# One planned order for four engines, or an order for each: dilated attention and the branch products of a two-layer block

## The chip, the cores and the metric

One core of one Trainium2 chip. The metric is the device time of one execution in microseconds (us). Before the change it is 3101.1 us, the median of three runs from 3099.65 to 3101.7.

## The reference, cut to what matters

The program is one layer of a mixing block and then one layer of a second block, on 1024 rows of 1024 columns in float32. The change touches a part of the first layer:

```python
qb, kb, vb = ...                        # columns of h @ w_in: 12 heads of 128, in 3 groups of 4
for gi, (window, dil) in enumerate(((128, 1), (512, 4), (2048, 16))):
    o_g, lse_g = _dilated_group(qb[hs], kb[hs], vb[hs], bias[gi], dil, window // (2 * dil))
wgt = softmax(stack(lses), axis=0)      # over the 3 groups
o_b = sum(wgt[..., None] * stack(outs)) # the shares of the groups
merged = gate_a * (o_a @ w_branch_a) + gate_b * (o_b @ w_branch_b)
```

A dilated group is attention in a band: a tile of 128 queries sees up to 256 keys at its dilation, with a bias, a maximum, an exponential and a product with the values.

## The kernel before, in words

Every engine runs a program of its own, and semaphores tie them. Each large matmul is split in three: a float32 operand is cut into a rounded high part and a rest, and `mm3` (L2499 to L2502) issues high*high, high*low and low*high.

**The work of the stage.** It is written as threads, Python generators, each with a version for TensorE, ScalarE, VectorE and SP (the queue that issues the DMAs). `("v", g)` are the columns of the values of group g: `pe_cols` (L1633) makes 8 keys (four column tiles ct by two halves hf), a key being 24 matmuls of 512 columns in two steps of 12, written here as V3.1a and V3.1b for ct 3, hf 1. The two PSUM banks of these keys alternate, so a key waits until the key two before it has been taken out. ScalarE takes out half 0 (L1777), VectorE half 1 (L1919). Then TensorE turns the tile in two or three pieces into bank 7 (`turn`, L1667; R3.0 is piece 0 of ct 3), and VectorE copies each piece out (L1929) before the next may be turned: one bank holds them. `("qk", g)` are 16 keys of queries and keys, taken out by ScalarE (L1760). `("gb", 3)` are 8 keys of a gate (taken out at L1844).

`("att", g)` is the attention of the 8 tiles of a group. For tile i TensorE does the scores S (L1694), VectorE adds the bias, takes the maximum and negates it (L1871, L1875, L1877), ScalarE does four exponentials (L1798), TensorE turns the result T (L1717), ScalarE copies half of it (L1812 or L1817) and VectorE the other half (L1893 or L1899), TensorE multiplies with the values U (L1729), ScalarE copies the output (L1825) and SP stores it. The scores of tile i+1 are issued before T of tile i.

The weights of the column threads come through two slots: SP loads tile n+2 when the last key of tile n is done, ScalarE cuts out the high part (`act_w_split`, L1618), VectorE the low part (`dve_w_split`, L1623), in their places in the threads.

**The order.** `merged` (L76) lays the steps of several threads into one list: step j of n of a thread with the bounds a and b is due at a + (b-a)(j+1)/n, and the earliest due is next. `walk` (L89) goes through such a list and lets each named thread make one step. Four engines walk the same list, each with its own version of the threads:

```python
plan_dil = [merged((("v", 0), 20, 0.0, 44.0), (("att", 0), 34, 36.0, 148.0), ...)]   # L1580
def pe_dilated(t):
    for order in plan_dil:
        walk(order, lambda key: {...}[key[0]](t, key[1]))                             # L1739
```

**The stage behind it.** `plan_br` (L2052) does the same with two threads on TensorE, ScalarE and VectorE. `("br", 0)` is the first branch product: 16 keys of 24 matmuls, of which the first four run together over all of k, fed by the loaded `oT` as ScalarE (L1831) and VectorE (L1835) cut it. VectorE multiplies each with its gate (L2225), for which the load of `mT` must have landed, and splits the next weights (L1623). `("cb",)` weighs the three groups: VectorE's shares (L2175 to L2192) and sums (L2205, L2208, L2211) with GpSimd's help, then eight turns on TensorE (L2104, K0 to K7), whose results ScalarE (L2127) and VectorE (L2169) split. The second branch product waits for the last of them. SP loads in the order of its program: `oT` 0 to 5 (at L2008, the first step of `("gb", 3)`), `oT` 6 and 7 (L2023), `mT` (L2027), the three groups' outputs (L2279), gates and weights.

Of the kernel before, what the change touches and what calls it, by code (L numbers as in the profile page):

```python
# [120 lines left out]
def program(nc, x, wst, wab, cwt, vecs, gate, relb, meta, lam, lruw, cst, onehot, rope, msk, out):  # L121
    with ExitStack() as ctx:
# [388 lines left out]
        for s in range(16):  # L511
            h, part = divmod(s, 2)
            threads = [(("inv", h, part), NINV, 0.0, 1.0)]
# [1043 lines left out]
        def tile_order(first, rest):  # L1557
            res = []
            for g in range(3):
                n = len(tiles(g))  # L1560
                res += [(g, 0, x_) for x_ in first]
                for i in range(n):
                    if i + 1 < n:
# [13 lines left out]
        TN = {k: n for n, k in enumerate(tile_list)}  # L1577

        steps_att = lambda g: 4 * len(tiles(g)) + 2
        plan_dil = [merged((("v", 0), 20, 0.0, 44.0), (("att", 0), 34, 36.0, 148.0), (("v", 1), 20, 44.0, 136.0),  # L1580
                           (("qk", 1), 33, 134.0, 228.0), (("att", 1), 34, 227.0, 348.0), (("v", 2), 20, 228.0, 335.0),
                           (("qk", 2), 33, 333.0, 425.0), (("att", 2), 34, 424.0, 492.0), (("gb", 3), 18, 424.0, 489.0))]


        gbst = [A(BIAS1 + 512 * i, 512) for i in range(4)]
# [149 lines left out]
                yield from pe_cols(t, key, GB0 + key[1], key[2], key[3])  # L1735

        def pe_dilated(t):
            for order in plan_dil:
                walk(order, lambda key: {"qk": pe_qk, "v": pe_v, "att": pe_att, "gb": pe_gb}[key[0]](t, key[1]))  # L1739

        def act_qk(a, g):
            dil = DIL[g]
# [108 lines left out]
            act_o_high(a, 1)  # L1851

        def act_dilated(a):
            for order in plan_dil:
                walk(order, lambda key: {"qk": act_qk, "v": act_v, "att": act_att, "gb": act_gb}[key[0]](a, key[1]))

        def dve_att(v, g):
            todo = tiles(g)
# [94 lines left out]
            dve_o_low(v, 1)  # L1953

        def dve_dilated(v):
            for order in plan_dil:
                walk(order, lambda key: {"qk": dve_qk, "v": dve_v, "att": dve_att, "gb": dve_gb}[key[0]](v, key[1]))

        def sp_qk(sp, g):
            if g == 1:  # L1960
# [54 lines left out]
                    w_load(sp, GB0 + 2 + c)  # L2015

        def sp_dilated(sp):
            for order in plan_dil:
                walk(order, lambda key: {"qk": sp_qk, "v": sp_v, "att": sp_att, "gb": sp_gb}[key[0]](sp, key[1]))
            for kt in (6, 7):  # L2020
                sp.wait_ge(att_mm, (2, kt, "t"))
                sp.wait_ge(oa_in, kt - 6)
                sp.do.dma_start(oT[:, kt, :], sc_o[kt]).then_inc(*oa_in.tick(kt - 5))  # L2023

            sp.wait_ge(att_mm, (2, 7, "s"))
            for cb in range(4):
                sp.do.dma_start(mT[:, 2 * cb:2 * cb + 2, :], sc_h[2 * cb:2 * cb + 2].rearrange("a p n -> p a n")).then_inc(*ga_in.tick(cb))  # L2027
# [21 lines left out]
        br_mm = flow("br_mm", br_keys)  # L2049
        br_done = flow("br_done", br_keys)  # L2050
        br_prod = flow("br_prod", [k for k in br_keys if k[0]])
        plan_br = merged((("br", 0), 17, 0.0, 1.0), (("cb",), 18, 0.28, 1.0))  # L2052
        BA0, BB0 = 42, 46

        def br_bank(k):
# [50 lines left out]
                yield  # L2106

        def pe_branches(t):
            walk(plan_br, lambda key: pe_cb(t) if key[0] == "cb" else pe_br(t, 0))
            for _ in pe_br(t, 1):  # L2110
                pass

# [36 lines left out]
        def act_branches(a):  # L2149
            for kt in range(2, 8):  # L2150
                act_o_high(a, kt)
            walk(plan_br, lambda key: act_cb(a) if key[0] == "cb" else act_br0(a))
            for k in br_keys[16:]:
                _, cb, ct, hf = k
                hs = slice(512 * hf, 512 * hf + 512)
                a.wait_ge(br_done, k)
                a.do.activation(m_hi[2 * cb + ct][:, hs], mT[:, 2 * cb + ct, hs], ACT.Copy).then_inc(*turned_hi.tick(("m", *k[1:])))
                if BN[k] in (17, 20):
                    act_w_split(a, 48 if BN[k] == 17 else 49)
                if BN[k] in (23, 25, 27, 30):  # L2160
                    act_wo_high(a, {23: 50, 25: 53, 27: 51, 30: 52}[BN[k]])
# [66 lines left out]
        def dve_branches(v):  # L2228
            for kt in range(2, 8):
                dve_o_low(v, kt)  # L2230
            walk(plan_br, lambda key: dve_cb(v) if key[0] == "cb" else dve_br0(v))
            def low(k):
                _, cb, ct, hf = k
                hs = slice(512 * hf, 512 * hf + 512)
# [1719 lines left out]
```

## Time and profile before

| | us |
|---|---|
| median of 3 runs | 3101.1 |
| the profiled execution's own time | 3101.83 |
| its span, first to last instruction | 3099.9 |
| TensorE busy | 3013.0 |
| VectorE busy | 1558.6 |
| ScalarE busy | 1072.9 |
| mean granted TensorE clock, share of full | 0.990 |

Times of the trace count from the start of the span. The dilated stage lies from about 1080 to 1577 us, the branch products to about 1724 us. The idle time of TensorE is what a better order could take away; matmuls overlap, so the busy time of a group is not its length, and the number of matmuls over a busy stretch gives the rate. The granted clock is 1.00 at 2.4 GHz and 0.50 at 1.2 GHz.

### The profile page before, as it was taken

The page shows a single profiled execution, that of the slowest core. Times are in us where ns is not written, and L with a number is a line of the kernel's source. Part 1 is how long each engine was busy: PE and PEld are TensorE (multiplying, and loading weights), DVE is VectorE, ACT ScalarE, POOL GpSimd, SP SyncE. Part 2 cuts the span into 40 slices and gives each one's busy share as a digit, 9 for nine tenths or more (in the row PEclk, how much of TensorE's full clock was granted, in tenths as well). Part 3 has the DMA queues.
Part 4 walks back from the last instruction along what each step waited for, and adds up shares of the span by engine and source line. Part 5 has one row for each costly group of instructions (what it writes and reads, how often), then busy time and mean ns, then how long its engine had stood idle before and what let it go on. Part 6 is the DMA issues. An engine that isn't in the chain of part 4 may idle for free.

```text
span 3099.9 us, 39140 instructions
## 1 busy us (share of the span) xinstructions
PE 3013.0 (97%) x16315; PEld 2530.8 (82%) x16315; DVE 1558.6 (50%) x2184; ACT 1072.9 (35%) x2306; POOL 366.3 (12%) x433
## 2 busy tenths in 40 slices
PE   7999999999999999999999999999999999999998
PEld 5788888888888877877878888888888888888887
DVE  5566666667653224032147545444454488643453
ACT  4443453454442213232332341112111244314453
POOL 0122232232231000000000000000000022001111
PEclk9999999999999999999999999999999999998999
DMA  3211111111112111111263321111111141102001
GB/s 120 69 51 52 42 55 48 35 42 35 35 45 65 41 58 52 45 42 55 101 226 110 124 100 61 41 55 41 55 54 42 62 140 41 55 28 76 28 28 42
DMA packets 59649, 193.37 MB, mean 62 GB/s; under 512 B 7728, under 2 KB 15536, under 8 KB 50256
## 3 DMA queue, kind: packets, MB, share of 16 engines
q1 hardware_dynamic: 58464, 189.26, 17.7%
q8 instruction: 129, 2.11, 0.3%
q10 hardware_dynamic: 1008, 1.61, 0.2%
q14 instruction: 48, 0.39, 0.0%
HBM read 156.86 MB, written 33.98 MB: 62 GB/s over the span
## 4 chain that ended last, share of the span: by engine, by line
PE 87%; DVE 7%; ACT 3%; issue 1%; DMA 1%; POOL 0%; SPq 0%; ACTq 0%; POOLq 0%; DVEq 0%
PE ps L2500 22%; PE ps L2502 22%; PE ps L2501 21%; PE ps L728 3%; PE ps L734 3%; PE ps L1729 2%; PE ps L3382 1%; PE ps L3445 1%; PE ps L740 1%; PE ps L771 1%; PE ps L765 1%; PE ps L1694 1%; PE ps L759 1%; PE ps L711 1%; PE ps L780 1%
## 5 line engine op out<-in xcount | busy, mean ns | idle before, releaser
L2500 PE MATMUL ps<-r,r 128*128 128x512 f32 (+3 forms) x2992 | 1172.6, 392 | 24.9 <-DVE ar L3630 4.4
L2502 PE MATMUL ps<-r,r 128*128 128x512 f32 (+3 forms) x2992 | 1114.0, 372 | 0.0
L2501 PE MATMUL ps<-r,r 128*128 128x512 f32 (+3 forms) x2992 | 1112.0, 372 | 0.0
L2500 PEld LDWEIGHTS ps<-r,r 128*128 128x128 f32 x2992 | 564.7, 189 | 118.5 <-issue 19.7
L2502 PEld LDWEIGHTS ps<-r,r 128*128 128x128 f32 x2992 | 562.9, 188 | 99.9
L2501 PEld LDWEIGHTS ps<-r,r 128*128 128x128 f32 x2992 | 565.2, 189 | 81.1 <-issue 2.5
L2500 PE MATMUL ps<-r 128*128 128x512 f32 x512 | 199.7, 390 | 0.8 <-DVE r L2489 0.8
L2502 PE MATMUL ps<-r 128*128 128x512 f32 x512 | 199.2, 389 | 0.0
L2501 PE MATMUL ps<-r 128*128 128x512 f32 x512 | 199.2, 389 | 0.0
L2761 DVE TENSOR_TENSOR ar<-ar,ps 128x512 f32<-128x512 f32 x224 | 150.8, 685 | 89.7 <-PE ps L2502 89.6
L2484 ACT ACTIVATE r<-ar 128x2048 fp32r<-128x2048 f32 x48 | 91.7, 1910 | 268.1 <-PE ps L2502 252.3
L1237 DVE COPY_PREDICATED ar<-mk,ar 128x512 f32<-128x512 uint8 x80 | 79.5, 994 | 135.2 <-ACT ar L1029 134.9
L2489 DVE TENSOR_TENSOR r<-ar,r 128x2048 fp32r<-128x2048 f32 x48 | 109.8, 2288 | 55.5 <-ACT r L2484 55.5
L1623 DVE TENSOR_TENSOR r<-ar,r 128x2048 fp32r<-128x2048 f32 (+1 forms) x24 | 50.9, 2120 | 168.5 <-ACT r L1618 168.5
L2708 DVE TENSOR_TENSOR ar<-ar 128x512 f32<-128x512 f32 x64 | 44.3, 691 | 173.7 <-ACT ar L2640 173.7
L1357 POOL TENSOR_SCALAR ar<-ar 128x128 f32<-128x128 f32 x128 | 100.8, 799 | 205.3 <-PE ps L771 205.3
L1137 DVE SCALAR_TENSOR_TENSOR ar<-ar 128x1024 f32<-128x1024 f32 x96 | 123.1, 1282 | 1.6
L728 PEld LDWEIGHTS ps<-ar 128*128 128x128 f32 x768 | 96.9, 191 | 29.1 <-DVE ar L1241 15.4
L1024 ACT ACTIVATE ar<-ps 128x512 f32<-128x512 f32 x96 | 57.4, 598 | 178.4 <-PE ps L728 178.4
L728 PE MATMUL ps<-ar 128*128 128x128 f32 x768 | 106.5, 281 | 11.2 <-DVE ar L1241 6.5
L2500 PEld LDWEIGHTS ps<-r 128*128 128x128 f32 x512 | 96.1, 188 | 21.0 <-DVE r L2489 1.2
L2502 PEld LDWEIGHTS ps<-r 128*128 128x128 f32 x512 | 96.1, 188 | 20.0
(325 smaller groups left out, 3968.8 us busy)
## 6 DMA issues: line engine op xcount, KB each, us to landing
ar<-wst SPq DMA_DIRECT2D x72, 1024.0 KB, 4.8
ar<-wst SPq DMA_DIRECT2D x56, 512.0 KB, 3.9
ar<-x SPq DMA_DIRECT2D x16, 512.0 KB, 5.7
ar<-sc_g SPq DMA_DIRECT2D x32, 256.0 KB, 4.6
sc_h<-ar SPq DMA_DIRECT2D x32, 256.0 KB, 2.1
sc_x<-ar SPq DMA_DIRECT2D x16, 512.0 KB, 2.7
ar<-sc_x SPq DMA_DIRECT2D x16, 512.0 KB, 4.3
sc_b<-ar SPq DMA_DIRECT2D x24, 260.0 KB, 2.0
```

What stands on the lines that cost most here:

```text
L728: o = t.do.matmul(q4(bank(4), j), q4(MT, j), mixed(FB0, b, j), start=True, stop=True)
L734: o = t.do.matmul(q4(bank(3), j), q4(Yb, j), mixed(BT, b, j), start=True, stop=True)
L1137: o = v.do.scalar_tensor_tensor(out=tmp, in0=r_[:, j:j + 1024], scalar=w[:, j:j + 1], in1=tmp, op0=ALU.mult, op1=ALU.add)
L1237: v.do.copy_predicated(mixed(BT, b), blocked(mk[:, n, :], b), blocked(Xb if n < 6 else bank(3), b)).then_inc(*inv_dve.tick(k(("XT", n))))
L1357: o = p.do.tensor_scalar(q4(kd[g % 2], d), q4(sqk[q], c), db[q][d][:, POS[c]:POS[c] + 1], None, ALU.mult)
L1729: o = t.do.matmul(q4(bank(6), hh), PT3[0:m, 2 * hh + j, :], Vt[g][0:m, ci, 128 * hh:128 * hh + 128], start=(j == 0), stop=(j == len(parts) ...
L2484: a.do.activation(w_set(j)[0], place, ACT.Copy).then_inc(*w_hi.tick(j))
L2489: v.do.tensor_tensor(lo, w_slot(W2 + j)[0], hi.bitcast(F32), ALU.subtract).then_inc(*w_lo.tick(j))
L2500: t.do.matmul(o, l[0], r[0], start=first, stop=False)
L2501: t.do.matmul(o, l[0], r[1], start=False, stop=False)
L2502: return t.do.matmul(o, l[1], r[0], start=False, stop=last)
L2761: v.do.tensor_tensor(dst, dst, bk, ALU.add).then_inc(*ff2_acc.tick(k))
```

## The change

`own_orders` makes one list for each engine: the same threads, with bounds that an engine may shift (`DIL_LEANS`, `BR_LEANS`). The shared bounds change a little too. No instruction is added or taken away; each engine's list is put in another order.

```diff
-        plan_dil = [merged((("v", 0), 20, 0.0, 44.0), (("att", 0), 34, 36.0, 148.0), (("v", 1), 20, 44.0, 136.0),
-                           (("qk", 1), 33, 134.0, 228.0), (("att", 1), 34, 227.0, 348.0), (("v", 2), 20, 228.0, 335.0),
-                           (("qk", 2), 33, 333.0, 425.0), (("att", 2), 34, 424.0, 492.0), (("gb", 3), 18, 424.0, 489.0))]
+        DIL_THREADS = ((("v", 0), 20, 0.0, 44.0), (("att", 0), 34, 36.0, 148.0), (("v", 1), 20, 35.0, 136.0), (("qk", 1), 33, 117.0, 228.0), (("att", 1), 34, 225.0, 348.0), (("v", 2), 20, 210.0, 335.0), (("qk", 2), 33, 332.0, 425.0), (("att", 2), 34, 424.0, 492.0), (("gb", 3), 18, 420.0, 489.0))
+        DIL_LEANS = {
+            "pe": {("v", 0): (0.0, 2.0), ("att", 0): (0.0, -7.0), ("qk", 1): (0.0, -9.0), ("att", 1): (-1.0, -3.0), ("v", 2): (0.0, -2.0), ("qk", 2): (-15.0, 0.0), ("gb", 3): (0.0, 2.0)},
+            "act": {("att", 1): (11.0, 15.0)},
+            "dve": {("v", 2): (-7.0, 0.0)},
+            "sp": {},
+        }
+
+        def own_orders(threads, leans):
+            return {engine: merged(*[(k, n, a_ + by.get(k, (0.0, 0.0))[0], b_ + by.get(k, (0.0, 0.0))[1]) for k, n, a_, b_ in threads]) for engine, by in leans.items()}
+
+        plan_dil = own_orders(DIL_THREADS, DIL_LEANS)
...
         def pe_dilated(t):
-            for order in plan_dil:
-                walk(order, lambda key: {"qk": pe_qk, "v": pe_v, "att": pe_att, "gb": pe_gb}[key[0]](t, key[1]))
+            walk(plan_dil["pe"], lambda key: {"qk": pe_qk, "v": pe_v, "att": pe_att, "gb": pe_gb}[key[0]](t, key[1]))
...
-        plan_br = merged((("br", 0), 17, 0.0, 1.0), (("cb",), 18, 0.28, 1.0))
+        BR_THREADS = ((("br", 0), 17, 0.0, 1.0), (("cb",), 18, 0.31, 1.0))
+        BR_LEANS = {
+            "pe": {("br", 0): (0.0, -0.03), ("cb",): (-0.03, -0.03)},
+            "act": {("cb",): (0.0, -0.12)},
+            "dve": {("br", 0): (0.12, 0.09), ("cb",): (0.0, 0.12)},
+        }
+        plan_br = own_orders(BR_THREADS, BR_LEANS)
```

ScalarE, VectorE and SP walk `plan_dil["act"]`, `plan_dil["dve"]`, `plan_dil["sp"]` likewise, and `plan_br` is read by engine too. Worked out by the rule of `merged`, the lists differ in these places (S, T, U, V, R as above, with the tile or piece; V behind the last key of a group is the next group's; Q1 and Q2 are keys of `("qk", 1)` and `("qk", 2)`, G of `("gb", 3)`; half = L1919, copy = L1929, sum = L1871 to L1877, low = L1623, pv = L1893 or L1899, pa = L1812 or L1817, ev = taking a key out):

```
TensorE, end of ("v", 0)
 before  V3.1b R3.0 S0 R3.1 R3.2 S1 T0 V0.0a U0 V0.0b S2 V0.1a T1 V0.1b U1
 after   V3.1b S0 R3.0 V0.0a R3.1 S1 R3.2 V0.0b T0 V0.1a U0 S2 V0.1b T1 V1.0a
TensorE, end of ("v", 1)
 before  R2.2 V3.1b U5 S7 R3.0 T6 R3.1 R3.2 U6 Q1a T7 Q1b Q1a U7
 after   R2.2 U5 V3.1b S7 T6 Q1a R3.0 Q1b U6 R3.1 Q1a Q1b R3.2 T7 Q1a Q1b U7
TensorE, end of ("qk", 1) and of ("v", 2)
 before  Q1b S0 V0.0a S1 T0 V0.0b ...   V3.1b U5 R3.0 S7 T6 R3.1 U6 Q2a T7
 after   Q1b V0.0a V0.0b S0 V0.1a S1 ... V3.1b U5 R3.0 S7 T6 Q2a R3.1 Q2b Q2a U6
TensorE, ("gb", 3)
 before  Q2b S0 Ga S1 T0 Gb U0 ...   Ga Gb U6 T7 U7
 after   Q2b Ga S0 Gb S1 T0 Ga U0 ... Ga U6 Gb T7 U7
VectorE, ("v", 1) with ("att", 0), last steps
 before  sum7 half3 copy3.0 pv6 copy3.1 copy3.2 pv7 low
 after   half3 sum7 copy3.0 pv6 copy3.1 low copy3.2 pv7
ScalarE, start of ("qk", 2)
 before  pa7 ev o7 ev      after  ev exp7 o6 ev high ev pa7 ev o7
SP, ("qk", 1) and ("gb", 3)
 before  load store6 skew store7         after  skew load store6 store7
 before  load load oT store0             after  load oT load store
VectorE, branch stage
 before  gate0 low gate1-4 shares K0sum  after  gate0 low gate1-3 shares K0sum gate4
```

In the branch stage TensorE's list is the same as before; ScalarE's differs in one place.

## Rows read from the trace of the kernel before

**Rows 1.** The page: busy time by engine, and the chain by engine.

```profile
PE 3013.0 (97%) x16315; PEld 2530.8 (82%) x16315; DVE 1558.6 (50%) x2184; ACT 1072.9 (35%) x2306; POOL 366.3 (12%) x433
...
PE 87%; DVE 7%; ACT 3%; issue 1%; DMA 1%; POOL 0%; SPq 0%; ACTq 0%; POOLq 0%; DVEq 0%
```

**Rows 2.** Busy time by stretch: length, PE, PEld, DVE, ACT, POOL, clock, DMA, GB/s.

```profile
1135.00:1246.00 111.00, 100.27 (x543) 84.30 (x543) 43.30 (x54) 33.48 (x87) 0.00 (x0) 0.97 0.14 48
1246.00:1325.00 79.00, 78.93 (x348) 64.99 (x347) 9.17 (x4) 22.77 (x20) 0.00 (x0) 1.00 0.13 44
1325.00:1424.00 99.00, 95.76 (x481) 77.76 (x482) 35.17 (x46) 31.82 (x86) 0.00 (x0) 0.97 0.15 51
...
1511.00:1577.00 66.00, 62.76 (x354) 54.22 (x355) 18.67 (x28) 32.31 (x93) 0.00 (x0) 1.00 0.40 147
1577.00:1676.00 99.00, 93.30 (x426) 76.48 (x425) 61.61 (x96) 18.98 (x25) 11.69 (x8) 1.00 0.47 176
```

**Rows 3.** Whom TensorE waited for, 1090 to 1740 us: total, times, longest.

```profile
PE ps L1667 <- DVE ar L1929: 7.0, 5, 2.9
PE ps L1667 <- DVE ar L1919: 5.7, 3, 3.9
PE ps L2104 <- DVE ar L2211: 2.7, 1, 2.7
PE ps L1694 <- ACT ar L1760: 2.2, 2, 1.1
PE ps L2500 <- DVE r L1623: 1.5, 1, 1.5
PE ps L2500 <- DVE r L2169: 1.5, 1, 1.5
PE ps L1729 <- ACT ar L1817: 1.2, 1, 1.2
PE ps L2500 <- DVE r L1835: 1.1, 1, 1.1
```

**Rows 4.** Ten-microsecond stretches around four of the waits; columns as in Rows 2.

```profile
1136.00:1146.00 10.00, 6.39 (x31) 5.24 (x32) 3.65 (x6) 1.86 (x8) 0.00 (x0) 0.83 0.29 105
1222.00:1232.00 10.00, 5.37 (x31) 4.67 (x30) 5.22 (x8) 2.65 (x10) 0.00 (x0) 0.83 0.36 131
1412.00:1422.00 10.00, 9.66 (x32) 7.18 (x33) 1.57 (x3) 2.19 (x9) 0.00 (x0) 0.66 0.16 63
...
1608.00:1618.00 10.00, 7.33 (x35) 5.84 (x34) 9.17 (x14) 0.00 (x0) 5.80 (x4) 1.00 0.95 362
```

**Rows 5.** VectorE's timeline: start, length, line, work, idle before and releaser.

```profile
1138.09 0.96 DVE L1871 TENSOR_TENSOR ar<-ps,ar 128x768 f32<-128x768 f32 x1 [2.18 <-PE ps L1694]
...
1140.15 0.68 DVE L1929 COPY ar<-ps 128x512 f32<-128x512 f32 x1
...
1225.74 1.01 DVE L1919 COPY ar<-ps 128x512 f32<-128x512 f32 x1
```

**Rows 6.** TensorE's groups, 1135 to 1246 us, eight tiles of attention.

```profile
L1729 PE MATMUL ps<-ar 128*128 128x128 f32 (+1 forms) x128 | 18.4, 286 | 0.1
L1694 PE MATMUL ps<-ar 128*128 128x256 f32 (+1 forms) x64 | 15.4, 387 | 0.0
...
L1717 PE MATMUL ps<-ar 128*128 128x128 f32 (+1 forms) x64 | 9.2, 291 | 0.0
```

**Rows 7.** ScalarE's group of the exponentials, 1135 to 1246 us.

```profile
L1798 ACT ACTIVATE ar<-ar 128x256 f32<-128x256 f32 (+1 forms) x32 | 15.4, 485 | 9.9 <-DVE ar L1877 9.9
```

**Rows 8.** VectorE's group of the low parts, 1135 to 1246 us.

```profile
L1623 DVE TENSOR_TENSOR r<-ar,r 128x2048 fp32r<-128x2048 f32 x2 | 4.6, 2286 | 3.5 <-ACT r L1618 3.5
```

**Rows 9.** SP's timeline: the issue of the load of `oT` 0 to 5.

```profile
1511.23 0.39 SPq L2008 DMA_DIRECT2D ar<-sc_o  x1
```

**Rows 10.** VectorE's timeline in the branch stage: the start of the shares.

```profile
1606.53 0.17 DVE L2175 TENSOR_TENSOR ar<-ar 128x16 f32<-128x16 f32 x1
```

**Rows 11.** ScalarE's timeline in the branch stage: a weight's high part.

```profile
1619.38 1.92 ACT L1618 ACTIVATE r<-ar 128x2048 fp32r<-128x2048 f32 x1 [11.80 <-DMA ar<-wst]
```

More of the change, by code:

```diff
@@ L1853, in act_dilated @@
         def act_dilated(a):
-            for order in plan_dil:
-                walk(order, lambda key: {"qk": act_qk, "v": act_v, "att": act_att, "gb": act_gb}[key[0]](a, key[1]))
+            walk(plan_dil["act"], lambda key: {"qk": act_qk, "v": act_v, "att": act_att, "gb": act_gb}[key[0]](a, key[1]))
         def dve_att(v, g):
@@ L1955, in dve_dilated @@
         def dve_dilated(v):
-            for order in plan_dil:
-                walk(order, lambda key: {"qk": dve_qk, "v": dve_v, "att": dve_att, "gb": dve_gb}[key[0]](v, key[1]))
+            walk(plan_dil["dve"], lambda key: {"qk": dve_qk, "v": dve_v, "att": dve_att, "gb": dve_gb}[key[0]](v, key[1]))
         def sp_qk(sp, g):
@@ L2017, in sp_dilated @@
         def sp_dilated(sp):
-            for order in plan_dil:
-                walk(order, lambda key: {"qk": sp_qk, "v": sp_v, "att": sp_att, "gb": sp_gb}[key[0]](sp, key[1]))
+            walk(plan_dil["sp"], lambda key: {"qk": sp_qk, "v": sp_v, "att": sp_att, "gb": sp_gb}[key[0]](sp, key[1]))
             for kt in (6, 7):
@@ L2108, in pe_branches @@
         def pe_branches(t):
-            walk(plan_br, lambda key: pe_cb(t) if key[0] == "cb" else pe_br(t, 0))
+            walk(plan_br["pe"], lambda key: pe_cb(t) if key[0] == "cb" else pe_br(t, 0))
             for _ in pe_br(t, 1):
@@ L2151, in act_branches @@
                 act_o_high(a, kt)
-            walk(plan_br, lambda key: act_cb(a) if key[0] == "cb" else act_br0(a))
+            walk(plan_br["act"], lambda key: act_cb(a) if key[0] == "cb" else act_br0(a))
             for k in br_keys[16:]:
@@ L2230, in dve_branches @@
                 dve_o_low(v, kt)
-            walk(plan_br, lambda key: dve_cb(v) if key[0] == "cb" else dve_br0(v))
+            walk(plan_br["dve"], lambda key: dve_cb(v) if key[0] == "cb" else dve_br0(v))
             def low(k):
```

## The prediction

> **What bounds the kernel now.** First the page: TensorE is busy for 3013.0 of 3099.9 us and holds 87% of the chain that ends last [rows 1]. No order on another engine is worth anything unless it takes idle time from TensorE, and no instruction is removed. So the second view is TensorE's busy time by stretch [rows 2]: in the dilated stage it stands idle for 111 - 100.27 = 10.7 us while group 0 of the attention runs beside the values of group 1, 0.1 us under the keys of group 1, 3.2 us beside the values of group 2, 3.2 us in group 2 with the gate, and 5.7 us in the branch products. Together 23 us; that is the ceiling from waits. The third view says whom it waited for [rows 3]: eight waits for VectorE's copies before a turn (7.0 + 5.7 us), two for the last key before the first scores (2.2), two where the stages meet (1.2 + 1.1), three in the branch products (1.5 + 2.7 + 1.5). The fourth is the clock [rows 4]: around three of these waits the granted clock falls to 0.83, 0.83 and 0.66 over ten microseconds, with both levels (2.4 and 1.2 GHz) in each stretch. That loses 1.7 + 1.7 + 3.4 = 6.8 us, of which I put some 0.7 into time in which TensorE stood idle anyway, so 6.1 on its work. Waits and clock together: 29 us, under 1%.
>
> **How I price the new order.** I follow it with durations of rows. A step of 12 matmuls is 12 x 78.93/348 = 2.72 us [rows 2]. A tile of group 0 takes about 15.4/8 = 1.9 us for S, 1.2 for T, 2.3 for U [rows 6], a little less without the slow clock. VectorE needs 2.1 us for a sum of an edge tile (1138.09 to the copy at 1140.15) and 2.5 for a wide one by the same rule, 0.7 for a copy, 1.0 for half a key [rows 5], 2.3 for a low part [rows 8]; ScalarE (15.4 + 6.0 for the read of the sums)/8, about 2.3 with its gaps, for a tile's exponentials [rows 7]. A wait vanishes when the work that TensorE now has between the trigger and the use is longer than the chain on the other engine.
>
> **End of the values of group 0.** Of the 10.7 us, 4.4 lie here, in three waits, 2.9 the longest [rows 3]. Before, R3.0, S0, R3.1, R3.2 stand behind each other, and VectorE runs the sum of S0 ahead of the copy that R3.1 waits for [rows 5]. After: S0 covers the half copy; V0.0a (2.7) stands before R3.1, and the sum plus the copy end 1.4 + 2.1 + 0.7 = 4.2 us after V3.1b, when TensorE is at 1.3 + 0.4 + 2.7 = 4.4. S1 covers the next copy. Waits gone: 4.4 us.
>
> **Middle and end of the values of group 1.** The other 6.3 us: before, two waits of 0.6 and 1.0 us at pieces in the middle, then 3.9 at R3.0 [rows 3] and 0.8 at R3.1, because half3 (at 1225.74) sits behind sum7 [rows 5]. After: VectorE does half3 before sum7, and T6 and a step of Q1 stand before R3.0, another step and U6 before R3.1, two steps before R3.2. Following all 24 pieces, the nearest are a copy that ends 0.1 us before the piece behind it, two that end 0.2 to 0.4 before it, and the last: a low part now stands ahead of copy3.2 and pv7, so these wait for ScalarE's high part of the next weight; queued behind it is U7 alone, which TensorE reaches as pv7 ends. Gain 6.3; I leave 0.6 us for such near misses. The cover is the columns: were one step shorter by half, each near miss would be a wait of about 1 us.
>
> **Group 1 with the values of group 2.** S0 no longer waits 1.1 us for the last key; V0.0a and b (5.4) cover the 1.1 that the copy takes. The 2.1 us before R3.1 go, as a step of Q2 stands there. On ScalarE pa7 is now behind the third key of Q2; behind it wait pv7 and U7, and TensorE has two more steps before U7, which just covers it. Gain 3.2.
>
> **Group 2 with the gate.** Ga covers the last key before S0: gain 1.1. At the end U6 has moved ahead of Gb, so ScalarE's o6 is done before the last key and pa7 comes 0.5 us sooner; U7 and the first branch product still wait. Of 2.4 us I leave 2.1. Gain 0.3.
>
> **SP.** The skew (four DMAs, for the bias of group 2) goes ahead of a weight load and a store; the weight load is later by the time between the end of V3.1b and the sum of S7, some 2.5 us, and its high part stands five steps of columns on (13.6 us). The store has its trigger later than the skew. The load of `oT`, issued at 1511.23 when the keys were done [rows 9], goes out some 20 us sooner, ahead of one weight load; that weight is first used behind eight steps of the gate, 21.8 us, and four tiles of attention. Both priced at nothing on TensorE; if the cover were gone, the price is a load's landing once, bounded by 0 and the 11.8 us that ScalarE waited for a weight load at another place [rows 11]; nearest is 0, with 21.8 us of cover against 11.8.
>
> **Branch products.** The list of TensorE is unchanged. VectorE starts the shares one gate sooner, now at 1606.53 [rows 10], so the 2.7 us before K0 shrink by something between 0 (if the loads of the groups' outputs are only then there) and 2.7. The weight behind K1 does not come sooner: its high part waits for a DMA until 1619.38 [rows 11], and then come ScalarE, a split and the low part. What K0 gains is mostly waited out there: I take 0.3. The 1.5 for the first low part stays, as `mT` lands when it did; so does the 1.5 after K7, whose chain has no cover in either order.
>
> **Lean costs.** TensorE changes between columns and attention work 125 times instead of 121, for which no row has a price: between 0 and the 0.3 to 0.4 us of one small matmul [rows 6]; I take 0.1 each, 0.4 us lost.
>
> **The clock.** Before each fall TensorE had stood idle: 4.4 us in pieces, 3.9, and 2.1. At 1608 to 1618 it stood idle for 2.7 us and the clock stayed 1.00 [rows 4], so not every such wait costs clock; the three that did are all ones that the new order removes. I take the 6.1 us as won.
> The Trainium skill (TensorE: Matmul & The Clock Gate, section A second HAM failure mode: psum-queue depth-cycling) says that short idles between groups of matmuls are enough to keep the clock swinging between its levels. By that the falls would outlive the long waits, and the sum would be 14.6 us as in the first rival; the 1.00 at 1608 to 1618 speaks against it.
>
> **The sum.** 4.4 + 6.3 + 3.2 + 1.1 + 0.3 + 0.3 + 6.1 = 21.7; less 0.6 and 0.4: 20.7 us. The profiled execution took 3101.83, so 3081.1; the median lies 0.7 lower, which gives **3080.5**.
>
> **The rivals.**
> *The clock falls all the same.* For it: S, T, U and short turns follow each other around the same spots in the new list too, and the longest fall, at 1412 to 1422 [rows 4], came after the shortest of the three waits. Against it: between the falls, with the same S, T and U and no wait, the stretches are at 1.00. Gain 20.7 - 6.1 = 14.6: 3086.5.
> *The near misses miss.* My hand count has margins of 0.1 to 0.4 us at some six pieces, on durations good to a few per cent. If each costs 1 us and two bring a fall of 1.7 us with them: 20.7 - 6 - 3.4 = 11: 3090. For it: VectorE's chain for a piece is as long as TensorE's work beside it. Against it: TensorE's own small gaps make it slower than I count, which helps.
> *A head of the queue in the wrong place: slower.* VectorE's half copies now stand ahead of pv in both value groups (half before pv1, half2 before pv4); where TensorE wants U before that key has ended, it waits for pv, pv for half, half for the key. That is a wait of up to 3.9 us as the longest now [rows 3] and 1.7 us of clock with it: 5.6. It decides from four such places on (22 us); six of the eight column tiles give 3101 + 13 = 3114. Against it: in the lists U stands behind the key's last step wherever half stands ahead of pv.
> *It does nothing.* The waits only move to other pieces, or a later stage waits anyway: 3101. Against it: after 1740 us TensorE waits on engines that follow it, not on a fixed time.
>
> **How the numbers follow.** Forecast 0.57, the clock rival 0.18, near misses 0.13, no effect 0.06, slower 0.06. About 0.2%, 6 us, is what a measurement of this kernel can tell from no change. Faster: 0.57 + 0.18 + 0.13 = 0.88; within 0.2%: 0.06; slower: 0.06. The range: downward, no near miss (0.6), half of the 5.7 us of the branch stage gone instead of 0.3 (2.5) and half of the 2.1 left before it (1.0), 4.1 us more: 3076; upward to just beyond the near misses, 3092.
>
> **What would show it.** TensorE's waits for VectorE's copies at L1667 fall from 12.7 us to under 1.5; no wait at L1694; idle time before the branch products about 2 us instead of 2.4; K0 waits less than 2.7 but a wait for a low part (L1623) appears behind K1; the clock is 1.00 in every stretch of the dilated stage; TensorE's busy time falls by some 5 us, as slow matmuls become fast ones. I am wrong if L1729 waits for VectorE, if the clock falls without a gap, or if a step of columns waits for a low part in the dilated stage.

## The result, and the profile after

The changed kernel took **3073.86 us** (median of four runs, 3072.83 to 3075.48), the kernel before 3101.3 (four runs, 3099.65 to 3101.7): ratio 0.991, 95% interval 0.9898 to 0.9923, 27.4 us less. The forecast was 20.7 us less, and its range ended at 3076, so the time lies below it. The direction and the mechanism held; the size did not. The profiled execution took 3072.83 us, where that of before took 3101.83: 29.0 us between the two traces.

The page, which answers to [rows 1]:

```profile
span 3071.0 us, 39141 instructions
...
PE 3000.5 (98%) x16315; PEld 2523.1 (82%) x16315; DVE 1557.9 (51%) x2184; ACT 1071.9 (35%) x2306; POOL 365.7 (12%) x433
...
PE 87%; DVE 7%; ACT 3%; issue 1%; DMA 1%; SPq 1%; POOL 0%; ACTq 0%; POOLq 0%; DVEq 0%
```

The same 16315 matmuls, and TensorE is busy for 12.5 us less. The mean granted clock rose from 0.990 to 0.994; 0.004 of 3071 us is 12.3, though three places make that good to some 3 us only. The matmuls are no fewer: most of the 12.5 us is time in which they now run at 2.4 instead of 1.2 GHz, and some 2 us are costs around the old waits that the profile counts as busy time (worked out below). The other engines do what they did.

Whom TensorE waited for from 1090 to 1740 us, with total, times and longest; it answers to [rows 3]:

```profile
PE ps L2511 <- DVE r L1632: 1.5, 2, 0.9
PE ps L2511 <- DVE r L2180: 1.5, 1, 1.5
PE ps L2115 <- DVE ar L2222: 1.2, 1, 1.2
PE ps L2511 <- DVE r L1843: 1.1, 1, 1.1
PE ps L1738 <- ACT ar L1825: 0.7, 1, 0.7
...
```

The lines moved by 8 to 11: the turns, L1667 before, are L1676, and the scores, L1694 before, are L1703. Neither appears any more: the eight waits for VectorE's copies (12.7 us) and the two for a last key (2.2) are gone. Before U7 0.7 us is left of 1.2 (L1738), before K0 1.2 of 2.7 (L2115). What stayed is the start of the branch products (L1843, 1.1), the first low part (L1632, 0.9 where it was 1.5), now with a second wait for a low part behind K1 (0.6), and the wait behind K7 (L2180, 1.5).

Busy time by stretch, columns as in [rows 2]. The stretches hold the same microseconds, not quite the same work, since the stage now ends some 25 us sooner:

```profile
1135.00:1246.00 111.00, 111.00 (x605) 94.10 (x604) 44.79 (x54) 38.35 (x91) 0.00 (x0) 1.00 0.16 55
1246.00:1325.00 79.00, 79.00 (x359) 65.87 (x358) 12.79 (x11) 23.66 (x27) 0.00 (x0) 1.00 0.12 47
1325.00:1424.00 99.00, 99.00 (x506) 80.58 (x505) 31.82 (x39) 31.86 (x81) 0.00 (x0) 1.00 0.12 41
```

TensorE is busy from end to end where it stood idle for 10.7 and 3.2 us, and the clock is 1.00 where it was 0.97.

**Where the 29.0 us went.** Four instructions mark the same points of the work in both kernels: ScalarE takes out the last key of `("qk", 0)`, of `("qk", 1)` and of `("qk", 2)`, and TensorE starts the first branch product; a fifth ends the branch products. Their timelines (start, length, line, work, idle before and releaser), first of the kernel before, then of the changed one:

```profile
1087.34 0.60 ACT L1760 ACTIVATE ar<-ps 128x512 f32<-128x512 f32 x1 [4.84 <-PE ps L2502]
1324.97 1.04 ACT L1760 ACTIVATE ar<-ps 128x512 f32<-128x512 f32 x1 [4.34 <-PE ps L2502]
1510.79 1.03 ACT L1760 ACTIVATE ar<-ps 128x512 f32<-128x512 f32 x1 [4.35 <-PE ps L2502]
1576.58 0.47 PE L2500 MATMUL ps<-r,r 128*128 128x512 f32 x1 [1.14 <-DVE r L1835]
1718.87 0.47 PE L2500 MATMUL ps<-r,r 128*128 128x512 f32 x1 [0.26 <-issue]
```

```profile
1085.48 0.60 ACT L1768 ACTIVATE ar<-ps 128x512 f32<-128x512 f32 x1 [4.84 <-PE ps L2513]
1308.23 1.10 ACT L1768 ACTIVATE ar<-ps 128x512 f32<-128x512 f32 x1 [4.34 <-PE ps L2513]
1486.89 1.09 ACT L1768 ACTIVATE ar<-ps 128x512 f32<-128x512 f32 x1 [4.35 <-PE ps L2513]
1550.81 0.47 PE L2511 MATMUL ps<-r,r 128*128 128x512 f32 x1 [1.14 <-DVE r L1843]
1691.88 0.47 PE L2511 MATMUL ps<-r,r 128*128 128x512 f32 x1 [0.26 <-issue]
```

From the differences, for these two and for the runs below:

| us between marks | to end of qk 1 | to end of qk 2 | to first branch product | branch |
|---|---|---|---|---|
| before | 237.63 | 185.82 | 65.79 | 142.29 |
| after | 222.75 | 178.66 | 63.92 | 141.07 |
| gain | 14.88 | 7.16 | 1.87 | 1.22 |

That is 25.1 us. The other 3.8 of the traced pair lie outside: 1.9 ahead of the first mark and 1.9 behind the last, where the change touches nothing. The clock differed there: from 20 to 40, 80 to 100 and 2640 to 2720 us it was 0.83, 0.91 and 0.98 before and 0.91, 1.00 and 1.00 after. It is spread, not the change: the changed kernel run again (`a1_again`) reads 0.83, 1.00 and 0.98 there, and takes 1382.1 us behind the last mark, where the first trace of it took 1379.1 and the kernel before 1381.0.

### The profile page after: what moved, and what is told of

Its sections match the earlier page's. It is cut to its first block, busy times and chain, and to the rows that moved or that the text cites. A ratio compares the mean times of both kernels' runs of the same rounds, so it can differ in the third digit from the quotient of the medians.

```text
span 3071.0 us, 39141 instructions
## 1 busy us (share of the span) xinstructions
PE 3000.5 (98%) x16315; PEld 2523.1 (82%) x16315; DVE 1557.9 (51%) x2184; ACT 1071.9 (35%) x2306; POOL 365.7 (12%) x433
## 4 chain that ended last, share of the span: by engine, by line
PE 87%; DVE 7%; ACT 3%; issue 1%; DMA 1%; SPq 1%; POOL 0%; ACTq 0%; POOLq 0%; DVEq 0%
PE ps L2511 22%; PE ps L2513 21%; PE ps L2512 21%; PE ps L728 3%; PE ps L734 3%; PE ps L1738 2%; PE ps L3393 1%; PE ps L3456 1%; PE ps L1703 1%; PE ps L740 1%; PE ps L771 1%; PE ps L765 1%; PE ps L759 1%; PE ps L711 1%; PE ps L780 1%
## 5 line engine op out<-in xcount | busy, mean ns | idle before, releaser
L2511 PE MATMUL ps<-r,r 128*128 128x512 f32 (+3 forms) x2992 | 1170.2, 391 | 25.7 <-DVE r L234 4.9
L1632 DVE TENSOR_TENSOR r<-ar,r 128x2048 fp32r<-128x2048 f32 (+1 forms) x24 | 50.9, 2119 | 138.7 <-ACT r L1627 138.7
```

The lines of the kernel that those rows point to most:

```text
L2511: t.do.matmul(o, l[0], r[0], start=first, stop=False)
```

## Which part holds the gain

Four kernels, each timed in three rounds on one chip, where the kernel before took 3101.27 us (19 runs). Edits, here and below, are against the changed kernel; dots stand for lines that are not shown.

**The dilated stage alone** (`e1_dil`): the changed kernel with the old order of the branch stage.

```diff
-        BR_THREADS = ((("br", 0), 17, 0.0, 1.0), (("cb",), 18, 0.31, 1.0))
-        BR_LEANS = {
...
-        }
+        BR_THREADS = ((("br", 0), 17, 0.0, 1.0), (("cb",), 18, 0.28, 1.0))
+        BR_LEANS = {"pe": {}, "act": {}, "dve": {}}
```

> The new lists in the dilated stage alone; the branch stage walks its old list. Theory 1 (the trace of the stage: everything from its first column to the first branch product got shorter by 23.9 us, and what the profiled pair differs by outside the two stages, 3.8 us, is spread between executions): 3101.3 - 23.9 = 3077.4 us, and the idle time of the branch stage at about 6 us as before. Theory 2 (the time outside the stages fell because of the change, through the clock or the loads): about 3074, nearly all of the 27.4. Theory 3 (my prices were right and the rest is spread): 3081.

3077.19 us (3074.9 to 3082.06), ratio 0.9925 (0.9908 to 0.9942): 24.1 us less. K0 waited 2.7 us as before, and the first three columns of the table read 222.75, 178.65 and 63.90.

**The branch stage alone** (`e2_br`): the old bounds and no leans in the dilated stage.

```diff
-        DIL_THREADS = ((("v", 0), 20, 0.0, 44.0), (("att", 0), 34, 36.0, 148.0), (("v", 1), 20, 35.0, 136.0), ...
+        DIL_THREADS = ((("v", 0), 20, 0.0, 44.0), (("att", 0), 34, 36.0, 148.0), (("v", 1), 20, 44.0, 136.0), ...
...
+        DIL_LEANS = {"pe": {}, "act": {}, "dve": {}, "sp": {}}
```

> The new lists in the branch stage alone. Theory 1: the branch stage gives the 1.2 us that the two traces show, 3100.1 us; the wait before K0 shrinks from 2.7 to about 1.2 us and a wait for a low part of 0.6 us appears behind K1. Theory 3, from the prediction: 0.3 us, 3101.0. Theory 2: some 2 us more than 1.2 would have to come from here if it does not come from the dilated stage: 3098.

3100.24 us, ratio 0.9993 (0.9984 to 1.0003): by the time alone no gain is shown. Its waits, 1090 to 1740 us:

```profile
PE ps L2506 <- DVE r L1627: 2.1, 2, 1.6
...
PE ps L2110 <- DVE ar L2217: 1.4, 1, 1.4
```

K0 gained 1.3 us, and a second wait for a low part took 0.5 of it back.

**Neither** (`e3_null`): separate lists for the engines with the old bounds everywhere.

```diff
...
+        DIL_LEANS = {"pe": {}, "act": {}, "dve": {}, "sp": {}}
...
+        BR_LEANS = {"pe": {}, "act": {}, "dve": {}}
```

> The new code with the old bounds and no shifts: one list per engine, all equal to the old one, so no instruction changes its place. Theory 1: 3101.3 us within 1 us, and its trace differs from that of before by up to 2 us ahead of the dilated stage and behind the branch stage, as executions do. Theory 2: the same time, but no such differences outside the stages, since only the new orders would bring them.

3101.44 us, ratio 1.0001 (0.9992 to 1.001). Writing the order as four equal lists is worth nothing; the gain is all in the new places.

**Group 0 alone** (`eA_group0`): the new bounds of `v 1` and `qk 1` and TensorE's leans for `v 0`, `att 0` and `qk 1`, all else old.

```diff
...
-            "pe": {("v", 0): (0.0, 2.0), ("att", 0): (0.0, -7.0), ("qk", 1): (0.0, -9.0), ("att", 1): (-1.0, -3.0), ("v", 2): (0.0, -2.0), ("qk", 2): (-15.0, 0.0), ("gb", 3): (0.0, 2.0)},
-            "act": {("att", 1): (11.0, 15.0)},
-            "dve": {("v", 2): (-7.0, 0.0)},
+            "pe": {("v", 0): (0.0, 2.0), ("att", 0): (0.0, -7.0), ("qk", 1): (0.0, -9.0)},
+            "act": {},
+            "dve": {},
```

> The new bounds and shifts for the values of groups 0 and 1, the attention of group 0 and the keys of group 1 alone; the rest of the dilated stage and the branch stage as before. My prices: waits of 10.7 us and two of the three falls of the clock (3.0 us) go, 3101.3 - 13.7 = 3087.6 us. Theory 1, in which a wait costs TensorE more than its idle time (the busy time of the dilated stage fell by 8.4 us, where the clock explains 6.1 to 6.8): 10.7 + 3.4 + 1.2 = 15.3, 3086.0. The rival that the clock falls without the waits: two falls stay, 3090.6.

3087.73 us, ratio 0.9951 (0.9936 to 0.9966): 13.5 us less. By the time that is what my prices gave (3087.6) and not what a dearer wait gave (3086.0), but its interval, some 10.5 to 19.8 us, holds both. The marks decide: its stretches are 222.75, 185.76 and 65.78, the whole gain of the first (14.8 to 17.3 us against the five traces of the old order) and nothing of the others. TensorE's waits of the later groups stand as they were (2.1 us at R3.1, 2.2 in two waits at the scores, 2.7 before K0).

So the gains of the groups add up, each in its own stretch. Two things were not tried. No kernel lets one engine alone walk a new list. And no kernel lets all four engines walk one list with the new shared bounds: how much of the gain those bounds would give without any lean, and so what an order for each engine adds to a better order for all, stays open. The lists also differ in more places than the section on the change names (VectorE's and ScalarE's order beside the values of groups 1 and 2, and VectorE's later gates), and the single shifts were not priced.

## What a wait costs, and when the clock falls

Four kernels put waits back into the changed one, in TensorE's program behind U of a tile. They were run once each, since the marks read their cost to a tenth of a microsecond. The first two have five waits in group 0 and five in group 1.

**Short waits** (`g1_gap_out`): TensorE waits there for ScalarE's copy of the output.

```diff
+                if g < 2 and 1 <= i <= 5:
+                    t.wait_ge(att_o, (g, i))
```

> The new lists, and TensorE waits, after the value product of tiles 1 to 5 of groups 0 and 1, until ScalarE has copied that tile's output: ten waits put in, each about 0.7 us (the copy takes 0.6). Theory 1 (a short wait costs its idle time and no more, the clock does not fall): about 7 us more than the changed kernel's 3073 to 3076, the granted clock 1.00 from 1100 to 1500 us. Rival (short idles between groups of matmuls are enough to make the clock fall): 7 us and several falls of 1.7 to 3.4 us, 12 us or more in all.

3090.57 us. One of the waits on TensorE's timeline, then the stretch in group 0 and the one in group 1, columns as in [rows 2]:

```profile
1161.95 0.50 PE L2513 MATMUL ps<-r,r 128*128 128x512 f32 x1 [0.69 <-ACT ar L1835]
...
1155.00:1220.00 65.00, 61.56 (x353) 52.87 (x352) 29.55 (x36) 23.15 (x56) 0.00 (x0) 1.00 0.11 38
...
1345.00:1405.00 60.00, 56.57 (x265) 46.10 (x266) 18.64 (x24) 16.50 (x44) 0.00 (x0) 0.90 0.13 42
```

Two things are to be seen. In group 0 the clock stays at 1.00, and five waits of 0.69 us lengthen the first stretch of the table from 222.75 to 227.53: 4.78 us, or 0.96 for each. **A wait costs 0.27 us more than its idle time here.** In group 1 the same five waits bring the clock to 0.90, and the second stretch grows by 10.24 us, 5.4 more than the waits.

Where the 0.27 us come from can be read from the starts of the matmuls. U and the key behind it, first with the wait (the first matmul of the key is the line of 1161.95 above), then in the changed kernel:

```profile
1159.32 1.95 PE L1738 MATMUL ps<-ar 128*128 128x128 f32 x16
...
1162.29 0.40 PE L2514 MATMUL ps<-r,r 128*128 128x512 f32 x1
```

```profile
1158.22 1.95 PE L1738 MATMUL ps<-ar 128*128 128x128 f32 x16
1159.92 0.47 PE L2511 MATMUL ps<-r,r 128*128 128x512 f32 x1
1160.24 0.39 PE L2512 MATMUL ps<-r,r 128*128 128x512 f32 x1
```

Without a wait the key starts 1.70 us behind the start of U, 0.25 before the 1.95 us of U are over: matmuls overlap. The profile counts idle time from the end of U, so it leaves that overlap out (it models the ends; the comparison below needs the starts alone). From U to the second key matmul it is 2.97 us with the wait and 2.02 without: 0.95, of which 0.69 is idle time. At a turn the same reading gives less. A turn that waited in the kernel before, then one that does not wait in the changed kernel; the key matmuls ahead of them start at 1172.56 and 1162.53:

```profile
1173.55 0.63 PE L1667 MATMUL ps<-ar 128*64 128x128 f32 x4 [0.60 <-DVE ar L1929]
1174.01 1.04 PE L1717 MATMUL ps<-ar 128*128 128x128 f32 x8
```

```profile
1162.76 0.60 PE L1676 MATMUL ps<-ar 128*64 128x128 f32 x4
1163.19 1.03 PE L1703 MATMUL ps<-ar 128*128 128x256 f32 x4
```

From the key matmul to the work behind the turn it is 1.45 us against 0.66: 0.79, of which 0.60 is idle time. So a wait at a turn costs some 0.20 us beyond its idle time. For the scores it is some 0.26: the overlap of 0.16 with the key ahead, and 1.57 us for the eight matmuls of S behind a wait (at 1326.06 in the kernel before) against 1.46 without one (at 1211.33 in the changed kernel).

**Long waits** (`g2_gap_store`): TensorE waits for the store of the output.

```diff
+                if g < 2 and 1 <= i <= 5:
+                    t.wait_ge(att_saved[n % 2], (g, i))
```

> The same ten places, but TensorE waits until the output has been stored: copy 0.6, issue 0.3, landing 2.1 to 2.4, so 3.1 us each, as long as the longest waits of the kernel before. Theory 1 (long waits bring the falls of the clock with them): 31 us of idle time and a fall behind most of the ten, at 1.7 to 3.4 us each: 45 to 65 us more than the changed kernel. Rival (the falls came from the mix of work, not from the waits): 31 to 34 us, clock 1.00.

3120.16 us, 47.8 more in the first two stretches. The waits, then the clock in both groups:

```profile
PE ps L2513 <- DMA sc_b<-ar: 16.7, 6, 3.0
PE ps L1703 <- DMA sc_b<-ar: 8.3, 3, 2.9
PE ps L1676 <- DMA sc_b<-ar: 3.1, 1, 3.1
...
1155.00:1235.00 80.00, 66.22 (x345) 56.00 (x344) 28.87 (x34) 23.12 (x56) 0.00 (x0) 0.91 0.09 30
...
1360.00:1440.00 80.00, 65.73 (x282) 53.61 (x283) 21.18 (x28) 17.10 (x45) 0.00 (x0) 0.81 0.12 43
```

28.1 us of idle, ten times 0.27, and 17.0 left for the clock.

**One long wait** in group 1 (`g5_one_gap_g1`), and one in group 0 (`g6_one_gap_g0`):

```diff
+                if (g, i) == (1, 3):
+                    t.wait_ge(att_saved[n % 2], (g, i))
```

> The changed kernel with one wait put in, 2.7 us after the value product of tile 3 of group 1. If one wait of that length is enough for a fall there: 3.0 us and a fall of 1.7 to 3.4 us behind it, clock under 1.00 within 10 us. If it takes several: 3.0 us and clock 1.00.

> The same one wait after tile 3 of group 0, where five waits of 0.7 us did not make the clock fall and those of group 1 did. If the work around it decides: 3.0 us and clock 1.00 here, a fall in the run before. If only the length of the wait does: the same as in the run before.

3079.82 and 3079.41 us; the wait is 2.7 us in each. The 20 us around it, first in group 1 of the one:

```profile
1360.00:1380.00 20.00, 17.27 (x74) 14.27 (x74) 6.42 (x7) 3.88 (x8) 0.00 (x0) 0.83 0.04 14
```

and in group 0 of the other:

```profile
1180.00:1200.00 20.00, 17.28 (x86) 14.40 (x85) 5.66 (x8) 6.36 (x20) 0.00 (x0) 0.91 0.04 15
```

The stretches grew by 5.72 and 4.43 us. Less 2.97 for the wait, 2.75 and 1.46 are the clock's. One wait of 2.7 us in this stage was enough for a fall in each of the two executions, and a fall can cost as much as the wait.

## How near the near misses are

**VectorE's copy twice** (`g3_copy_twice`) **and three times** (`g4_copy_thrice`): the copy of each turned piece, L1938, is issued again behind itself.

```diff
+                v.do.tensor_copy(Vt[g][0:m, which, 128 * ct:128 * ct + 128], bank(7)[0:m, 0:128 * n].rearrange("p (c n) -> p c n", c=n)).then_inc(*dve_step.tick())
+                v.wait_ge(dve_step, dve_step.n)
```

> The new lists, and VectorE copies every turned piece of the values twice (0.7 us more for each of 32 pieces), so each piece's bank is free 0.7 us later. If the new order has the margins of 0.1 to 0.4 us that the prediction counted at some six pieces, TensorE waits there again, about 0.3 to 0.6 us each, 2 to 4 us in all. If the cover is wider than counted (the trace of the changed kernel shows no wait at these pieces at all): under 1 us.

> As the one before with three copies: 1.4 us more for each piece. With the margins of the prediction: waits of about 1 to 1.3 us at six pieces and shorter ones at others, 8 us or more and perhaps a fall of the clock. With a cover of a whole step of 12 matmuls (2.7 us) at most pieces: under 4 us.

3075.43 and 3088.62 us. Their waits from 1080 to 1540 us, first with two copies:

```profile
PE ps L1676 <- DVE ar L1938: 1.1, 3, 0.5
```

then with three:

```profile
PE ps L1676 <- DVE ar L1940: 4.5, 6, 1.2
```

A copy of about 0.7 us more on each piece makes three waits of at most 0.5 at the turns (and two of 0.4 and less ahead of U, 0.7 together), and the first two stretches grow by 2.5 and 0.6 us with the clock at 1.00. So the nearest pieces have 0.2 to 0.3 us to spare, and most have more than 0.7. One copy more, and the longest wait is 1.2 us, the clock falls to 0.91 from 1240 to 1260 and from 1380 to 1400 us, and the stretches are 8.7 and 3.7 us longer.

## The same programs again

`a1_again` is the changed kernel as it is, in five rounds.

> The changed kernel once more, with more rounds, on another chip or at another time. The traces give 25.1 us for the two stages (23.9 dilated, 1.2 branch). Theory 1 (the 27.4 us of the first four runs hold 2.3 us of spread outside the stages, where the same instructions took 1085.4 to 1088.9 us to the first dilated column in traces so far): 3101 - 25 = 3076 us, ratio 0.9919. Theory 2 (before loses more clock in the typical execution than in the one first profiled, as the trace of the kernel with equal lists showed, 10.2 us in three falls against 6.8): 27 to 28 us, ratio 0.9912.

It took 3075.98 us (3073.59 to 3078.49) against 3104.35 for the kernel before, ratio 0.991 (0.9895 to 0.9925), 28.4 us less. Its first three stretches are 222.75, 178.65 and 63.93, as after.

`n2_null` and `n3_null` are `e3_null` again, on a further chip.

> The kernel with equal old lists, looked at again. If the three falls of the clock in the old order vary from one execution to the next (6.8 us lost in the profile of before, 10.2 in the first look at this kernel): the stretch from the first dilated column to the end of the keys of group 1 takes 237 to 240.5 us, not always the same, where the new lists took 222.7 in every trace so far; time 3100 to 3105. If 10.2 belongs to this program and 6.8 to the program of before: again 240.0.

> The same again, for the spread: the first dilated column is issued somewhere between 1085 and 1089 us, if that is chance; always at 1087 or later, if the new lists of the dilated stage have to do with the 1085.4 to 1086.6 seen in nearly all of their traces.

They took 3102.17 us (ratio 0.9996, 0.9987 to 1.0006), and 3101.56 in a single run. While the new order reads the same in every trace, the old one does not: its first stretch is 237.63 (before), 240.03 (`e3_null`), 240.08 (`e2_br`, the same dilated stage), 237.54 and 238.03. The clock around the old waits in the kernel before:

```profile
1140.00:1160.00 20.00, 18.35 (x84) 14.54 (x85) 7.50 (x12) 5.13 (x18) 0.00 (x0) 0.91 0.04 14
1220.00:1240.00 20.00, 15.37 (x93) 13.63 (x92) 6.44 (x9) 4.14 (x12) 0.00 (x0) 0.91 0.28 93
1400.00:1420.00 20.00, 17.90 (x86) 13.97 (x85) 6.49 (x11) 6.94 (x21) 0.00 (x0) 0.86 0.23 80
1420.00:1440.00 20.00, 20.00 (x92) 16.14 (x91) 2.94 (x2) 4.99 (x5) 0.00 (x0) 0.97 0.04 14
```

and in `e3_null`:

```profile
1140.00:1160.00 20.00, 16.85 (x71) 13.14 (x72) 6.59 (x11) 5.13 (x18) 0.00 (x0) 0.83 0.08 33
1220.00:1240.00 20.00, 15.33 (x84) 13.48 (x83) 6.37 (x9) 5.18 (x16) 0.00 (x0) 0.83 0.25 81
1400.00:1420.00 20.00, 17.82 (x96) 14.48 (x95) 10.42 (x13) 6.34 (x20) 0.00 (x0) 0.96 0.20 67
1420.00:1440.00 20.00, 20.00 (x85) 15.94 (x85) 0.68 (x1) 3.85 (x6) 0.00 (x0) 0.87 0.04 16
```

The falls take 20 x (0.09 + 0.09 + 0.14 + 0.03) = 7.0 us in the one and 20 x (0.17 + 0.17 + 0.04 + 0.13) = 10.2 in the other, from one and the same order. The first mark moves as well, in both kinds of kernel: 1085.48 after, 1086.62 in `a1_again`, 1087.34 before, 1086.04 and 1088.94 in two nulls, 1088.88 in `eA_group0`, which has new lists. So those 3.5 us are spread of the stretch ahead of the change, not the change. To some 0.6 us they go with the clock there: where the mark is at 1085.48 and 1086.04, it was 0.91 from 20 to 40 us and 1.00 from 80 to 100; at 1086.62, 0.83 and 1.00; at 1087.34, 0.83 and 0.91; at 1088.88 and 1088.94, 0.83 and 0.83.

The branch stage, too, does not read the same in every trace of one order. In `n3_null` TensorE waits 2.7 us before K0 as in the kernel before, where the clock stayed at 1.00 [rows 4]; here it fell, and the branch stretch took 143.02 us, where the other three of the old order took 142.08 to 142.29:

```profile
1610.00:1620.00 10.00, 7.35 (x29) 6.13 (x30) 6.02 (x8) 2.40 (x2) 3.50 (x3) 0.83 0.59 229
```

## What is left in the branch products

**Half of the second product** (`b1_half_ready`). The second branch product waits for all eight low parts of the weighed groups (K0 to K7), while the keys of the first half of the rows read only the first four.

```diff
                 if sec:
-                    t.wait_ge(o_lo, 7)
+                    t.wait_ge(o_lo, 7 if k[3] else 3)
```

> The changed kernel with one edit: TensorE's keys of the second product that read only the first half of the rows wait for the first four of the eight turned tiles. The wait of 1.5 us behind K7 goes and nothing else moves: 1.8 us less than the changed kernel, 3074 us where that takes 3076, ratio 0.9905; the wait before K0 stays at 1.2 to 1.4 us, where it grew to 2.5 in the kernel with both edits.

3073.27 us (3072.87 to 3074.37), ratio 0.9907 (0.989 to 0.9923). Waits, 1090 to 1740 us:

```profile
PE ps L2511 <- DVE r L1843: 1.1, 1, 1.1
PE ps L2115 <- DVE ar L2222: 1.1, 1, 1.1
...
```

The 1.5 us behind K7 are gone, and the branch stretch is 138.85 us against 141.07 and 141.61 in the two traces of the changed kernel. It gained 2.2 or 2.8, where the wait and its 0.27 make 1.8. Six more traces of the same branch stage (`e2_br`, `g1_gap_out`, `g3_copy_twice`, `g4_copy_thrice`, `g5_one_gap_g1`, `g6_one_gap_g0`) read 140.25 to 141.83: 138.85 lies below them all, by 1.4 to 3.0 us. **It is the best version here by its trace.** It was not run on one chip with the changed kernel, and the two ratios to the kernel before overlap, so 2 us of total time is read from the marks alone.

**The first low part sooner as well** (`b2_half_low`): VectorE's low part of the second weight also moves ahead of the first gate.

```diff
-                if BN[k] in (1, 6, 10, 14, 15):
+                if BN[k] in (0, 6, 10, 14, 15):
...
```

> The changed kernel with two edits in the branch stage. TensorE's keys of the second product that read only the first half of the rows wait for the first four of the eight turned tiles, not for all; and VectorE splits the second weight tile ahead of the first gate, not behind it. The wait of 1.5 us behind K7 and that of 0.9 us before the second weight tile should go, each with the 0.27 us that a wait costs beyond its idle time, if a cover of one key (24 or 12 matmuls) is enough: 2.9 us less than the changed kernel. If the wait before K0 only grows by what comes earlier (the shares wait for a load): 1.8 us less.

3074.05 us, ratio 0.9904 (0.9888 to 0.9921), beside `a1_again` on the same chip at 3075.98: the 1.9 us between them are within the spread of both. What the trace adds: TensorE's wait before K0,

```profile
PE ps L2115 <- DVE ar L2222: 2.5, 1, 2.5
```

and VectorE's first share, which began in the changed kernel at

```profile
1578.67 0.18 DVE L2186 TENSOR_TENSOR ar<-ar 128x16 f32<-128x16 f32 x1 [3.18 <-DMA ar<-sc_b]
```

and here at

```profile
1578.68 0.18 DVE L2186 TENSOR_TENSOR ar<-ar 128x16 f32<-128x16 f32 x1 [5.16 <-DMA ar<-sc_b]
```

No wait for a low part is left, but K0 waits for 2.5 us instead of 1.1 to 1.4. TensorE and VectorE are both there sooner; the shares wait for the load of a group's output, which lands when it did. The clock falls to 0.91 between 1580 and 1600 us, and the branch stretch is 140.12, 1.3 us more than with the one edit. The wait only moved, and its owner is a load.

## Why the prediction was wrong in size

No wait at the turns or the scores and no fall of the clock in the stage survived, so the mechanism was right. The size was not: several terms were too small, all on the same side, and the largest is the price of a removed wait.

- **The waits by idle time: right.** 4.4 + 6.3 us in group 0 were to go, and 10.7 went; of 3.2 in group 1, 3.2 went; 1.1 + 0.3 behind it came out as 1.1 + 0.5. No wait moved to another piece. `eA_group0` shows the first of these alone.
- **The price of a removed wait: the first step that failed.** I priced each at its idle time and what it costs beyond that at nothing. By the starts of the matmuls it is 0.20 us more at a turn and 0.26 at the scores: eight turns and two scores make 2.1 us that the sum lacks. The stretches confirm it: the third gained 1.87 = 1.12 + 0.49 + 0.26, and the second 7.16 = 1.13 + 2.10 + 0.26 + 0.20 + 3.47, where the clock's rows give 3.4.
- **The near misses: deducted, and not there.** 0.6 us of the sum. `g3_copy_twice` shows that the margins were as small as I counted, 0.2 to 0.3 us; they held. With 1.4 us more on VectorE for each piece, as in `g4_copy_thrice`, the rival of the near misses is what happens.
- **The switches: deducted, and not seen.** The first stretch gained 14.88 = 10.73 + 7 x 0.20 + 2.75, and the clock should give 1.7 + 1.7 - 0.7 = 2.7. Nothing is left for the 0.4 us that I took for them.
- **The clock: right on average by mechanism, read too closely.** In the traced pair the falls gave back 2.7 + 3.5 = 6.2 us, the forecast. But the falls of the old order are no fixed cost: they took 7.0 us of the trace that I read and 10.2 of another. Over four traces of the old order (before and the three nulls) the four stretches take 632.3 us together, and 631.5 in that of before: 0.8 us more was to be won from the mean of these than from the trace I read.
- **The branch: 0.3 was too little.** K0 shrank from 2.7 to 1.2 us and a wait for a low part appeared behind K1, as foretold, but it took 0.5 us. What is left of K0's wait is the load of a group's output, as the shares of `b2_half_low` show: the end of my bounds where "the loads of the groups' outputs are only then there" came true in part. The stretch is 141.07 and 141.61 with the new order, and 142.4 in the mean of the four old ones: about 1.0 us, 0.7 more than forecast. Over the further traces it runs from 140.25 to 141.83 with the new order and from 141.71 to 143.02 with the old, so the 1.0 is rough. The 1.5 us behind K7 and the 1.1 ahead of the stage stayed; the first low part, which I held fixed at 1.5, took 0.9 to 1.8 with the old lists and 0.9 to 1.6 with the new.
- **SP at nothing: right.** No wait for a DMA stands in the list after, and the earlier load of `oT` brought nothing either.
- **A slip without effect.** (15.4 + 6.0)/8 is 2.7, not 2.3; the reads overlap the exponentials, and a tile of them takes 1.9 to 2.1 us on ScalarE's timeline before. No term hangs on it.

Put together: 20.7 + 2.1 + 0.6 + 0.4 + 0.2 + 0.8 + 0.7 = 25.5 us, and the marks give 25.7 between the old traces (632.3) and the two of the new order (606.7). The medians differ by 27.4 us here, 28.4 in `a1_again` and, without the branch order, 24.1 in `e1_dil`: 25.7 with a spread of about 2 from the stretches ahead and behind, where the first mark alone moved by 3.5 us with the clock at the start. So of the 6.6 us between the forecast and the median some 5 are these terms; the rest is not shown to be the change.

The range was wrong for the same reason: its lower end, 3076, held half of the branch stage, but no term for what a wait costs beyond its idle time, and the clock of one execution only.

Of the rivals, the clock's was the one worth its chance. The changed kernel has no fall, so here it did not come true; but `g1_gap_out` shows that its mechanism exists: with waits of 0.69 us and no longer one, the clock was 0.90 in group 1. The Trainium skill (TensorE: Matmul & The Clock Gate, section A second HAM failure mode: psum-queue depth-cycling) says that frequent short idles between groups of matmuls make the clock swing. The row of group 1 agrees, and that of group 0, 1.00 with the same five waits, does not. What in the work around them makes the difference, or whether it is chance, stays open: each row is one execution. The 1.00 at 1608 to 1618 with which I argued against this rival was one execution as well; `n3_null` lost clock at the same wait.

What I said would show it did: no wait at the turns and at the scores, 0.7 us before U7, a shorter K0 and a low part behind K1, clock 1.00. TensorE's busy time was to fall by 5 us and fell by 12.5, since some 2 us around the waits count as busy and the stretches at the start and from 2640 to 2720 us, too, ran at a higher clock in this trace.

## What to carry to other kernels

When one planned order serves several engines, look for the places where an engine repeats "produce, wait for the other engine, produce": a step of independent work between the trigger and the use takes the wait away without any new instruction. Price such a wait at its idle time, plus a measured fixed part (0.20 to 0.27 us here), plus the clock that it costs; read that fixed part from the starts of the matmuls, where the same work stands once with and once without a wait, or put known waits into the kernel. Before a fall of the clock goes into a sum, read it from several executions of the same program, and check the margins with a kernel that has one more copy on the tight engine.

## What the runs showed that was not expected

- A wait of TensorE costs about 0.27 us beyond the idle time that the profile shows (4.78 us for five waits of 0.69), and 0.20 at a turn. Most of it is overlap: without a wait a matmul starts 0.16 to 0.25 us before the end of the one ahead.
- The clock falls around single waits of 2.7 us in the attention (0.83 and 0.91 over 20 us), around five waits of 0.69 in group 1 (0.90 over 60 us) and not around the same five in group 0 (1.00). In the branch stage it stayed at 1.00 beside a wait of 2.7 us before [rows 4], fell to 0.83 over 10 us beside the same wait in `n3_null`, and to 0.91 over 20 us beside one of 2.5 in `b2_half_low`.
- One and the same order lost 7.0 or 10.2 us to such falls in two executions; the order without waits read 222.74 to 222.75 us for its first stretch and 178.65 to 178.66 for its second in all five traces of it.
